# Moving a depthwise conv tile from TensorE, and the sum of two tiles to GpSimd, in a two-layer decoder trunk

## The reference

```python
proj = einsum('bsd,de->bse', rms_norm(x, g), w_in)        # 1024 -> 5120
a, bv, bg, z = split(proj)                                # 1024, 1024, 1024, 2048 columns
ya = grouped_map(multiscale_pool(a)) * pool_scale         # windows 2, 4, 8, 16
u = bv * sigmoid(bg)
u = depthwise_causal_conv(u, conv_w, width=31) + conv_b   # one 31-tap filter per channel
yb = silu(layer_norm(u, cn_g, cn_b))
x = x + concat(ya, yb) * silu(z) @ w_out
```

## Time and profile before

| | |
|---|---|
| median of 3 runs | 367.87 us |
| span of the profiled execution | 365.8 us |
| TensorE busy | 360.4 us (99%) |
| VectorE busy | 270.0 us (74%) |
| ScalarE busy | 212.6 us (58%) |
| GpSimd busy | 17.0 us (5%) |
| granted clock of TensorE | full in all 40 slices |

### The profile page before, as it was taken

One profiled execution on the slowest core, in us unless ns is written; L12 is line 12 of the kernel. 1 busy time (PEld: TensorE's weight loads), 2 busy tenths in 40 slices (PEclk: granted clock), 3 DMA queues, 4 the chain that ended last, 5 costly groups with the idle time before them and its releaser, 6 DMA issues.

```text
span 365.8 us, 6403 instructions
## 1 busy us (share of the span) xinstructions
PE 360.4 (99%) x2545; PEld 335.2 (92%) x2545; DVE 270.0 (74%) x512; ACT 212.6 (58%) x421; POOL 17.0 (5%) x26
## 2 busy tenths in 40 slices
PE   8999999999999999999999999999999999999995
PEld 7999999999999999989999999999888888888885
DVE  3998789999989999939785998465664664665523
ACT  5769999664187561335656648538465465464510
POOL 0000000000000000000000000120111011010000
PEclk9999999999999999999999999999999999999999
DMA  7885063250505529034349064834442242000003
GB/s 290 342 337 232 1 231 141 98 222 7 225 10 222 231 81 374 7 115 177 168 154 421 2 231 124 337 116 137 167 151 92 102 154 87 38 0 2 1 2 115
DMA packets 8237, 54.33 MB, mean 149 GB/s; under 512 B 912, under 2 KB 1040, under 8 KB 1936
## 3 DMA queue, kind: packets, MB, share of 16 engines
q1 hardware_dynamic: 8064, 53.78, 38.6%
q10 hardware_dynamic: 144, 0.15, 0.2%
HBM read 52.88 MB, written 1.05 MB: 147 GB/s over the span
## 4 chain that ended last, share of the span: by engine, by line
PE 96%; DMA 2%; SPq 0%; DVE 0%; issue 0%
PE bank L931 23%; PE bank L932 21%; PE bank L933 21%; PE bank L963 15%; PE bank L988 6%; PE bank L1180 3%; DMA raw<-w 2%; PE bank L1161 2%; PE bank L1159 2%; PE bank L1168 1%; PE bank L1182 1%; PE bank L1140 1%; PE bank L1068 1%; PE bank L1005 1%; SPq L291 0%; DVE X L815 0%
## 5 line engine op out<-in xcount | busy, mean ns | idle before, releaser
L601 DVE TENSOR_TENSOR w_lo<-raw,w_hi 128x1024 fp32r<-128x1024 f32 x76 | 89.2, 1217 | 11.5 <-ACT w_hi L339 11.4
L339 ACT CAST w_hi<-raw 128x1024 fp32r<-128x1024 f32 x76 | 75.4, 1045 | 6.4 <-PE bank L933 4.6
L712 DVE SCALAR_TENSOR_TENSOR scratch<-scratch,params 128x256 f32<-128x256 f32 x142 | 59.1, 474 | 3.5 <-ACT scratch L437 3.3
L931 PE MATMUL bank<-h_hi,w_hi 128*128 128x256 f32 x208 | 60.0, 288 | 0.0
L933 PE MATMUL bank<-h_hi,w_lo 128*128 128x256 f32 x208 | 58.8, 283 | 0.0
L932 PE MATMUL bank<-h_lo,w_hi 128*128 128x256 f32 x208 | 58.8, 283 | 0.0
L931 PE MATMUL bank<-w_hi,h_hi 128*128 128x256 f32 x192 | 58.0, 302 | 0.0
L963 PE MATMUL bank<-H,raw 128*128 128x256 f32 x256 | 56.8, 379 | 0.7 <-DMA raw<-w 0.7
L963 PEld LDWEIGHTS bank<-H,raw 128*128 128x128 f32 x256 | 48.0, 190 | 7.1 <-DMA raw<-w 0.9
L932 PE MATMUL bank<-w_lo,h_hi 128*128 128x256 f32 x192 | 54.2, 282 | 0.0
L933 PE MATMUL bank<-w_hi,h_lo 128*128 128x256 f32 x192 | 54.1, 282 | 0.0
(11 more groups left out here) (120 smaller groups left out, 610.5 us busy)
## 6 DMA issues: line engine op xcount, KB each, us to landing
raw<-w SPq DMA_DIRECT2D x49, 1024.0 KB, 5.3
X<-xT SPq DMA_DIRECT2D x2, 512.0 KB, 5.0
out<-X SPq DMA_DIRECT2D x4, 256.0 KB, 2.6
consts<-const SPq DMA_DIRECT2D x1, 290.0 KB, 13.3
params<-vec ACTq DMA_DIRECT2D x1, 149.0 KB, 4.8
```

The costliest lines, as they stand in the source:

```text
L339: nc.scalar.copy(halves(w_hi, s % CUT, half), halves(raw, n % RAW, half)).then_inc(hi_cut, 1)
L601: nc.vector.tensor_tensor(halves(w_lo, s % CUT, half), halves(raw, n % RAW, half), halves(w_hi, s % CUT, half).bitcast(F32), ALU.subtract) ...
L712: nc.vector.scalar_tensor_tensor(V[:, c, :], U[:, c, k:k + S], column(CW + TAPS * c + k), V[:, c, :], ALU.mult, ALU.add).then_inc(tap, 1)
L931: nc.tensor.matmul(dst, wh, ah, start=start, stop=False, skip_group_check=True)
```

## The change

Conv tile 7 is no longer summed on TensorE. What served that goes: the two cuts of its weights, the 62 diagonals, the two cuts of `U`, `conv_taps` with its 93 matmuls and the way out of PSUM. Tiles 0 and 1 (`SIDE`) leave VectorE: after the first tap, ScalarE makes the products of taps 1 to 30 into a ring of four pairs (`SP_`, in the upper half of `SZ`), four taps in each slot from 3 to 9 and two in slot 10, and GpSimd adds each pair to `V` as one 128x512 tensor-tensor add, one after the other. ScalarE waits for all 30 adds before it writes the first gate of `ZB` into `SZ` (slot 12), and TensorE before the mean. VectorE keeps pairs (2, 3), (4, 5) and (6, 7). The plan takes, slot by slot, the pair with the most taps left, with a budget of 10 in every slot, and allows products from slot 8 on instead of 5. The new plan has 130 single taps and 25 pair adds, where the old one has 142 and 34.

```diff
-CONV_GROUPS = ((0, 1), (2, 3), (4, 5), (6,))
-CONV_PE = 7
-LEAD = 6
+SIDE = (0, 1)
+SIDE_FROM, SIDE_PER, SIDE_RING = 3, 4, 4
+CONV_GROUPS = ((2, 3), (4, 5), (6, 7))
...
+def side_taps(n):
+    i = (n - SIDE_FROM) * SIDE_PER
+    return range(i + 1, min(i + SIDE_PER + 1, TAPS)) if i >= 0 else ()
...
 def conv_plan():
...
+    left = {g: list(range(1, TAPS)) for g in range(len(CONV_GROUPS))}
+    before = None
     for n in range(BV[1], OA[0] + 1):
         plan[n] = []
-        budget = LONG_SLOT if n in (A[2] + 1, ZB[0] + 1) else SLOT
+        budget = SLOT
+        while budget > 0 or n == OA[0]:
+            here = [g for g in left if left[g] and CONV_GROUPS[g][0] // 2 < n // 2]
+            if not here:
+                break
+            g = max(here, key=lambda g: (len(left[g]) - (2 if g == before else 0), -g))
+            before = g
+            k = left[g].pop(0)
...
+            if k in PRODUCT_TAPS and tiles[0] // 2 < (n - 1) // 2 and A[0] <= n <= LAST_PRODUCT:
...
+        SP_ = SZ[:, KD:2 * KD, :].rearrange("p (b c) t -> p b c t", c=2)
...
+            for k in range(1, TAPS):
+                pool.wait_ge(side_ready, k)
+                if k == 1:
+                    pool.wait_ge(first_tap, 2)
+                else:
+                    pool.wait_ge(side_added, k - 1)
+                nc.gpsimd.tensor_tensor(V[:, 0:2, :], V[:, 0:2, :], SP_[:, (k - 1) % SIDE_RING, :, :],
+                                        ALU.add).then_inc(side_added, 1)
...
-            def build_diagonals(first, last):
...
+            def side_product(k):
+
+                if k > SIDE_RING:
+                    act.wait_ge(side_added, k - SIDE_RING)
+                for c in SIDE:
+                    last = nc.scalar.mul(SP_[:, (k - 1) % SIDE_RING, c, :], U[:, c, k:k + S], column(CW + TAPS * c + k))
+                last.then_inc(side_ready, 1)
...
+                for k in side_taps(n):
+                    side_product(k)
                 if n in A:
...
+                if n == ZB[0]:
+                    act.wait_ge(side_added, TAPS - 1)
                 if n in ZB or n in ZA:
...
-                if n in (A[2], ZB[0]):
-                    conv_taps(*((0, CONV_CUT) if n == A[2] else (CONV_CUT, TAPS)))
...
+            def channel_mean():
+                pe.wait_ge(side_added, TAPS - 1)
```

More of the change, by code:

```diff
@@ L97, in head_steps @@
     return scores, [s + to_turn for s in scores], [s + to_values for s in scores]
-CONV_GROUPS = ((0, 1), (2, 3), (4, 5), (6,))
-CONV_PE = 7
-CONV_CUT = 16
-BUILD = range(2, 8)
-PER_BUILD = 6
-LEAD = 6
+SIDE = (0, 1)
+SIDE_FROM, SIDE_PER, SIDE_RING = 3, 4, 4
+CONV_GROUPS = ((2, 3), (4, 5), (6, 7))
 PRODUCTS = 4
 LAST_PRODUCT = ZA[0] - 1
[L112 to L119, removed]
+def side_taps(n):
+    i = (n - SIDE_FROM) * SIDE_PER
+    return range(i + 1, min(i + SIDE_PER + 1, TAPS)) if i >= 0 else ()
 def conv_plan():
-    plan, last, used, count, rest = {}, {}, [], 0, conv_order()
+    plan, last, used, count = {}, {}, [], 0
+    left = {g: list(range(1, TAPS)) for g in range(len(CONV_GROUPS))}
+    before = None
     for n in range(BV[1], OA[0] + 1):
         plan[n] = []
-        budget = LONG_SLOT if n in (A[2] + 1, ZB[0] + 1) else SLOT
-        while rest and (budget > 0 or n == OA[0]):
-            g, k = rest[0]
-            tiles = CONV_GROUPS[g]
[L135 to L139, removed]
+        budget = SLOT
[6 more added lines that the diff above has]
+            k = left[g].pop(0)
+            tiles = CONV_GROUPS[g]
+            if k in PRODUCT_TAPS and tiles[0] // 2 < (n - 1) // 2 and A[0] <= n <= LAST_PRODUCT:
                 count += 1
@@ L273, in hybrid_trunk @@
         block = ctx.enter_context(nc.Block())
[L275 to L279, removed]
         def column(c, n=1):
@@ L385, in _ @@
             late_gate(0, 0, SG[:, :], ACT.Sigmoid, sig_ready)
-            def build_diagonals(first, last):
-                for k in range(first, min(last, TAPS)):
-                    for part, t in zip(diagonals(k), (taps_hi, taps_lo)):
-                        nc.scalar.mul(part, ident, t[:, k:k + 1].bitcast(F32)).then_inc(diag_ready, 1)
+            def side_product(k):
[4 more added lines that the diff above has]
+                last.then_inc(side_ready, 1)
             for n in range(1, OA[0] + 1):
@@ L1008, in square_sums @@
                     summed.then_inc(rms_sum, 1)
-            def conv_taps(a, b):
-                pe.wait_ge(ulo_ready, 1)
-                pe.wait_ge(diag_ready, 2 * b)
-                for k in range(a, b):
-                    last = product(bank[5][:, 0:S], diagonals(k), (u_hi[:, k:k + S], u_lo[:, k:k + S]),
-                                   k == 0, k == TAPS - 1)
-                last.then_inc(conv_done, 1)
             for n in range(PW):
@@ L1060, in _ @@
                     channel_step(n, k)
-            def channel_mean(tiles):
-                for c in tiles:
-                    if c == CONV_PE:
-                        pe.wait_ge(conv_out, 1)
-                    else:
+            def channel_mean():
+                pe.wait_ge(side_added, TAPS - 1)
+                for c in range(KD):
+                    if c not in SIDE:
                         pe.wait_ge(tap, TILE_DONE[c])
-                    last = nc.tensor.matmul(bank[1][:, 0:S], ones[:, :], V[:, c, :], start=(c == CONV_PE), stop=(c == 6),
+                    last = nc.tensor.matmul(bank[1][:, 0:S], ones[:, :], V[:, c, :], start=(c == 0), stop=(c == KD - 1),
                                             skip_group_check=True)
-                if tiles[-1] == 6:
-                    last.then_inc(mean_sum, 1)
+                last.then_inc(mean_sum, 1)
             pe.wait_ge(yp_ready, KD)
```

40 lines of the change are left out of this document (6 added, 34 removed).

## The result

The changed kernel takes 385.89 us, the median of 4 runs (385.1 to 386.79), against 367.88 us before: ratio 1.0492, interval 1.0472 to 1.0513, so 18 us slower. The forecast was 380.7 us, with a range of 356.5 to 391.

The account below looks back on a forecast made before the run. TensorE bound the kernel, VectorE close behind. VectorE's last tap at 145.3 plus 24 us of holds gave 169.3, the mean 170.7, 12.8 us later: span 378.6, plus 2.1 makes 380.7 us, range 356.5 to 391.

Parts of the forecast that it names:

- The removal: TensorE's two conv blocks of tile 7, all on the chain: 11.1 us go, mean reached at 146.8 instead of 157.91.
- The hold: GpSimd's adds against VectorE's two-operand instructions: each overlapping add costs VectorE 1.0 us, between bounds of 0 and 1.53.
- The number of adds that count: Of 30 adds, four cost nothing from 31 to 38 and two fit into waits; 24 cost VectorE 24 us.
- the waits of slots 6 and 8: VectorE waits there for ScalarE's first taps, 1.69 us each, about 3.4 together; two adds were to fit into them.
- What stands between the last tap and the mean: After the cut of unit 20, TensorE has 12.7 us left and VectorE 11.3: mean 1.4 us behind the last tap.
- the 3.6 us that VectorE "may lose": At the mean: VectorE's last tap ended by 154.29, TensorE arrived at 157.91, so VectorE had 3.6 us before TensorE waits.
- the diagonals' removal: ScalarE loses 62 diagonals at about 0.3 us; with its other changes -1.4 us, nothing on the path by itself.
- Without contention: Rival: adds beside VectorE cost it nothing, gain is whole: 356.8 us, up to 360; chance 0.22.
- The thin cover: Without contention, VectorE's last tap at 145.3 is only 1.5 us ahead of TensorE's 146.8 at the mean.
- Partial sharing: Rival: engines interleave and an add costs VectorE about half, 0.5 us: 368.7 us, range 361 to 375; chance 0.16.
- GpSimd as the bound: Rival: ScalarE waits for slow adds before unit 12's gate; decides from 2.8 us per add, 386 at 3.5; chance 0.10.
- contention at full length: Likeliest case: each overlapping GpSimd add holds VectorE for about its full length, 375 to 391 us; chance 0.52.

Follow-up runs that it names:

- the one-operand run: The changed kernel with each GpSimd add replaced by a 128x512 tensor-scalar multiply by 1, reading one operand: 369.18 us, ratio 1.0039.
- the memsets: The changed kernel with each GpSimd add replaced by a 128x1400 memset into its own buffer, which reads nothing: 360.75 us, ratio 0.98.

## Why the prediction was right, point by point

**The removal.** The steps on TensorE held: 93 matmuls are gone, 11.1 us. In the changed kernel they bought little, because the path was elsewhere: with the conv put back and without diagonals it is 2.8 us slower.

**The hold.** This decided the result and was right in kind, from one-sided evidence. I took 1.0 us per add between bounds of 0 and 1.53; measured are 1.03 us, and 0.48 us for half of it. That the two figures are so close is in part luck. I built the add from two or three passes of 0.84 ns per element, 1.68 or 2.52 ns; the slope of the hold is 2.15 ns per element, which is neither, and the 1.08 less 0.1 that I took was the middle of a wide span. The Trainium skill, "GPSIMD Engine Reference", section 3.1, gives 2.6 cycles per element for a two-input add; at the 1.2 GHz that the page reckons with, that is an estimated 2.17 ns. These runs agree, with 2.15 ns for the slope of both the adds and the hold. The exclusion between GpSimd's reads and VectorE's two-operand instructions, in "SBUF — State Buffer", section "Who interferes with whom" of the Trainium skill, is borne out by the alternation and by the memsets, which cost nothing. That the port is held for the whole instruction is not borne out by the one-operand run: 0.35 us held of 1.78. All VectorE instructions timed beside the adds read two operands from SBUF; what one with a single operand would do was not tested.

**The number of adds that count.** I counted 24 of 30. The first four, which I put at nothing, stretched the two cuts of unit 6 from 2.36 to 4.26 us (first row of VectorE's timeline), 1.9 us, and slot 4 began at 42.8 instead of 40.7. Their cover, VectorE's idling from 31 to 38, ended at 36.75 while the adds ran to 39.9: I had the length of the cover and not of the adds, which start only every 1.44 us. And no add vanished in the waits of slots 6 and 8: eight adds had ended by 55.7, and the next started at 64.58, behind the first tap that VectorE waited for as well. These are the terms that were too small: 26 x 1.03 instead of 24 x 1.0, and 1.9 us for the first four, 4.7 us together. Against them, the waits for first taps were 1.21 and 0.67 us instead of 1.69 each, 1.5 us less. The run with adds of 8 elements gives the total: the last tap ends at 146.3 there, where I had 145.3 without a hold, and at 172.9 here, where I had 169.3. So the 30 adds cost 26.6 us where I had 24, and 1.0 us was missing from the rest.

**What stands between the last tap and the mean.** I had 1.4 us behind the last tap, by way of the cut of unit 20. The mean came 2.5 us behind it, by way of the last pooled pair: its cut in slot 15 ended at 142.6, and from there TensorE had the last quarter of the pool map, units 17 to 20 and the first out unit without a break. The tie that I overlooked gives 1.1 us. It is the same one that stopped TensorE when its conv was taken out of the kernel before, so the 3.6 us that VectorE "may lose" were read at the wrong place; that slack did not enter the sum.

**The tail.** From the mean's start to the end it was 365.8 - 157.9 = 207.9 us before and 383.3 - 175.4 = 207.9 after. Nothing changed there, as forecast. The forecast span was 378.6, the measured 383.3: 3.6 us for the last tap and 1.1 us behind it. The median lies 2.6 us above the profiled span, against my 2.1.

**ScalarE.** The sum of its work changed by little, 212.6 to 211.3 us busy (forecast -1.4). But I called the diagonals' removal worth nothing on the path. Where the conv was put back they cost 3.9 us, standing in front of the cut of unit 6. In the sum for the changed kernel this did no harm.

**The rivals.** Without contention I had 356.8 us; with adds of 8 elements it is 358.5. The thin cover did tear: TensorE waited 1.5 us for a pooled cut, which it did not do before, while the 2.1 us for a weight unit from memory lie before 40 us, where it already waited 0.7. Partial sharing at 0.5 us is excluded by the hold of 1.03 us per add, GpSimd as the bound by the adds' 1.44 us. The price of the last one was wrong (see the run with one operand). The stated range of 356.5 to 391 would have held the opposite outcome too, so that the time lies in it says little; the narrower 375 to 391 for contention at full length, which I gave 0.52, holds it as well.

## What to carry to other kernels

An idle engine is not free work: ask whether its reads get in the way of the busy engine's, and price the move by what it holds of the busy engine, not by its own length. Here an add on GpSimd cost VectorE 1.03 us and the same add on VectorE itself 0.75. Where two engines are bound nearly equally, moving a small share from one to the other until both end together (12 of 31 taps, 1.2%) gave more here than moving all of it did, with GpSimd (385.9 us) or without (376.2). The slack is best measured by taking the work out, since waits that hang on the removed work go with it.

## What the runs showed of the hardware

GpSimd's one-operand multiply of 128x512 is slower than its two-operand add, 1.49 us alone against 1.26 to 1.30, and yet it holds VectorE for 0.35 us where the add holds it for 1.03. Small VectorE instructions wait for an add too: one of 128x2, usually 0.16 us, took 1.22.

TensorE's granted clock fell during the waits that VectorE's holds gave it. After an idle stretch of 7.4 us its matmuls started 0.21 us apart instead of 0.12; the window from 81.5 to 86 us has the clock at 0.50, which is 1.2 of 2.4 GHz:

```profile
80.78 0.55 PE L906 MATMUL bank<-h_hi,w_hi 128*128 128x256 f32 x1 [7.43 <-DVE w_lo L583]
81.12 0.42 PE L907 MATMUL bank<-h_lo,w_hi 128*128 128x256 f32 x1
81.34 0.42 PE L908 MATMUL bank<-h_hi,w_lo 128*128 128x256 f32 x1
```

```profile
81.50:86.00 4.50, 4.50 (x23) 4.50 (x22) 3.83 (x7) 3.60 (x9) 1.57 (x1) 0.50 0.64 229
```

It was back at 1.00 between 90 and 100 us, and fell again with the next long waits, of 6.6 us before 102.7 and of 3.1 us before 120.5: the windows of 100 to 107 and 120 to 124 us have 0.52 and 0.57. The stretch was bound by VectorE, so it should have cost little here. Where TensorE had no slack behind it, in the run with memsets, it cost 1.6 us.
